# Sixteen weight tiles, each loaded as 120 partitions and 8 partitions

## The chip, the cores and the metric

The kernel runs on one core of a Trainium2 chip. The metric is the device time of one execution in microseconds (us), the median over several runs. The core has a matrix engine (TensorE, PE in the profile), VectorE (DVE), ScalarE (ACT), GpSimd (POOL) and a queue engine SyncE (SP). Sixteen DMA engines carry all transfers between the memory of the chip (HBM) and the on-chip memory of 128 partitions (SBUF). Transfers are issued from SP, from ACT or from POOL, and all go to the same sixteen engines.

## The reference

One sequence of 256 tokens, width 1024, float32 all through, goes through two transformer blocks. The first has a gated feed-forward network, a token mixer (gated linear attention and blocked softmax attention) and another feed-forward network. The second has a mixer of a gated delta rule and an mLSTM, cross-attention to 256 memory tokens, and at its end a layer of 16,384 single-row experts (PEER). The change is in that last layer:

```
q = (rmsnorm(h, w) @ wq) as 8 heads of 2 x 128
scores of each half against 128 sub-keys; the 16 best of each half; the 16 best of their 256 sums -> 16 expert ids for each head and token
h += sum over heads and their 16 ids of  gate * act(u[id] . x) * v[id]
```

The weight `peer_wq` (1024 x 2048) gives the queries. Each token picks 8 x 16 = 128 experts, and each expert has one row u and one row v of 1024 floats, stored side by side as one row of `peer_uv`.

## The kernel before

Each engine has one instruction stream, written out in order by Python when the kernel is built. Buffers and semaphore counts are planned at that time too.

**Weights.** Almost all weights come as tiles of 128 partitions x 1024 floats (512 KB, one row of 4 KB for each partition), issued by SP in one list. The last part of that list is `TAIL` (line 181 of the code): 8 tiles of the second mixer's output weight, 8 of the cross-attention query weight, 8 of its output weight, and from index `T_PQ` = 24 on the 16 tiles of `peer_wq`. `PLACE[i]` says in which buffer tile i lands (`tail_slot(i)`), `FREED[i]` which earlier tile held that buffer. SP waits until that one has been used, and then issues one transfer (line 2874). A tile's semaphore is one of 16, `tail{i % NLAND}`. `land(...)` books 16 counts for a transfer, and `at(...)` gives the count that stands for it.

**The expert layer.** Tokens are worked on in two halves of 128 (r = 0, 1) and 8 heads: sixteen steps q = 8 r + head. `peer_tile(q)` (line 1216) multiplies the normed tokens with two tiles of `peer_wq` (indices 24 + 2 head and 25 + 2 head) into PSUM, 16 matmuls. It waits for each tile's semaphore. The tiles stay in place for the second half of the tokens. `peer_keys(q)` scores the sub-keys, and VectorE picks the sixteen expert ids.

**The gathers.** For each q and each of its 16 ids, POOL issues an indirect DMA (line 2831) which brings one row of `peer_uv` (8 KB) for each of the 128 tokens into one of nine buffers. There are 256 gathers. VectorE multiplies the u half with the token and sums (line 2131), ScalarE makes a gate and writes a diagonal matrix (line 2700), and TensorE adds the diagonal times the v half to an accumulator, four passes of 512 columns with weight loads (line 1313). That frees the buffer, and POOL issues a gather into it. The order of all this on TensorE and VectorE is the list of `peer_order()`. The routing of step q + 1 and later (tile, keys, top 16) is slotted between the gathers of step q. The matmul of line 1133 belongs to the output projections before it (the mixer's, the cross-attention's), and in part still runs beside the first gathers.

**The order at the change.** SP issues the 16 tiles of `peer_wq` as the buffers come free, while the cross-attention ends and the first gathers run. After them SP has only the output to write.

Of the kernel before, what the change touches and what calls it, by code (L numbers as in the profile page):

```python
# [23 lines left out]
NLAND = 16  # L24
# [9 lines left out]
class Book:  # L34
# [23 lines left out]
    def land(self, name, *key):  # L58
        return self.step(name, key, 16)

    def at(self, name, *key):
        return self.sem(name), 1 if self.known is None else self.known[(name,) + key]
# [119 lines left out]
T_OUT, T_XQ, T_XO, T_PQ = 0, 8, 16, 24  # L182
# [87 lines left out]
def program(nc, D, out, stack, book):  # L270
    up, at, land = book.up, book.at, book.land
# [147 lines left out]
    def raw_slot(j):  # L419
        return raw[:, (j % NRAW) * SLOT:(j % NRAW + 1) * SLOT]  # L420
# [5 lines left out]
    def tail_slot(i):  # L426
        k = PLACE[i]
        if k < NRAW:
            return raw_slot(items + k)
        if k >= 14:  # L430
            return extra[k]
        k -= NRAW
        return (whi32, wlo32)[k // NSPL][:, k % NSPL * SLOT:(k % NSPL + 1) * SLOT]
# [2411 lines left out]
    def sync_engine():  # L2845
        s = nc.sync
        for j, (kind, name, *i) in enumerate(stream):
            if j >= NRAW:
                k = j - NRAW
                if stream[k][0] == "w":  # L2850
                    s.wait_ge(*at("lo", k))
                elif stream[k][0] == "mod" and stream[k][2] == 0 and stream[k][3] < NMOD:
                    s.wait_ge(*at("ada_t", "shift", stream[k][3]))
                elif stream[k][0] in SUMS:
                    s.wait_ge(*at("ada", k))
                else:
                    s.wait_ge(*at("br", 2 * (raws.index(k) // 2) + 1))
            src = D[name][GATES.index(i[0]), i[1]] if kind == "ada" else D[name][MODS.index(i[0]), i[1]] if kind == "mod" else D[name][i[0]]
            s.dma_start(raw_slot(j), src).then_inc(*land(f"raw{j % NRAW}", j))
        for i, (name, _, k) in enumerate(TAIL):  # L2860
            j = FREED[i]
            if i < NRAW:
                s.wait_ge(*at("lo", items + i - NRAW))
            elif PLACE[i] < 14 and j is None:
                s.wait_ge(*at("tile", split_at[len(split_at) - 1 - (len(split_at) - 1 - (PLACE[i] - NRAW)) % NSPL]))
            elif j is None:
                s.wait_ge(*at("stage_t", 1, 0))
            elif j % 4 < 3:
                s.wait_ge(*at("used", j))
            elif T_XQ <= j < T_XO:  # L2870
                s.wait_ge(*at("xa_t", "q", 1, (j - T_XQ) // 4))
            else:
                s.wait_ge(*at("rows", "xa" if j >= T_XO else "mixed", j // 4 % 2, 1))
            s.dma_start(tail_slot(i), D[name][k]).then_inc(*land(f"tail{i % NLAND}", i))
        o3 = out.rearrange("(r p) n -> p r n", p=128)
        for r in range(2):
            for n in range(2):
                c = slice(n * 512, (n + 1) * 512)
                s.wait_ge(*at("last", r, "out") if n else at("last_sq", r, "out"))
                s.dma_start(o3[:, r, c], h[:, r, c]).then_inc(*land("out", r, n))  # L2880
        s.wait_ge(*at("out", 1, 1))
# [3 lines left out]
    scalar_engine()  # L2885
    gpsimd_engine()
    sync_engine()


# [131 lines left out]
```

## Time and profile before

| | us |
|---|---|
| median of 3 runs (lowest, highest) | 1637.08 (1636.48, 1638.92) |
| span of the profiled execution | 1635.0 |
| TensorE busy | 1492.0 (91%) |
| VectorE busy | 1054.2 (64%) |
| ScalarE busy | 721.3 (44%) |
| GpSimd busy | 332.9 (20%) |
| chain of waits: share of TensorE, of DMA | 57%, 24% |

The span runs from the first to the last instruction of the profiled execution. The device time of a run has some two microseconds around it. The page divides the span into 40 slices of 40.9 us and gives the busy share of each engine in tenths. The DMA line is the mean over the sixteen DMA engines. In the chain of waits each piece is what released the next, back from the last instruction.

### The profile page before, as it was taken

The numbers are of one execution on the slowest core, as the hardware profiler recorded it, in microseconds if no ns is written. First come the engines' busy times: TensorE is split into PE (matmuls) and PEld (weight loads), VectorE is DVE, ScalarE is ACT, GpSimd is POOL, SyncE is SP. The second block draws the span as 40 slices with busy tenths as digits, with TensorE's granted clock in tenths as the row PEclk, the third lists the DMA queues.
The fourth block names the chain that finished last, engine by engine and source line by source line (L and its number), as shares of the span: only waits on it lengthen the run. The fifth ranks groups of instructions, "written<-read, shape, count | busy, mean of one in ns | idle before, by whom it ended". The sixth has DMA issues, their size and how long they took to land.

```text
span 1635.0 us, 21410 instructions
## 1 busy us (share of the span) xinstructions
PE 1492.0 (91%) x7868; PEld 1099.5 (67%) x7868; DVE 1054.2 (64%) x1959; ACT 721.3 (44%) x1579; POOL 332.9 (20%) x324
## 2 busy tenths in 40 slices
PE   6999999999999999999999989988988888888786
PEld 6899998889899998999996665444433433334222
DVE  5677775756666556659652276667677677676644
ACT  4445455454454345645331243444444444444443
POOL 0200010000010001000001033434444444444441
PEclk9999999999999999899999999999999999999999
DMA  8989884447567656333325379999999999999995
GB/s 327 393 284 315 290 308 136 155 122 278 206 200 236 219 186 215 121 117 108 103 87 196 139 320 338 404 421 420 422 421 421 420 422 421 422 421 421 419 422 239
DMA packets 91738, 470.48 MB, mean 288 GB/s; under 512 B 10864, under 2 KB 11024, under 8 KB 58096
## 3 DMA queue, kind: packets, MB, share of 16 engines
q0 software_dynamic: 40096, 284.39, 42.7%
q1 hardware_dynamic: 50688, 183.52, 32.5%
q8 instruction: 63, 1.03, 0.3%
q10 hardware_dynamic: 848, 1.18, 0.2%
q14 instruction: 43, 0.35, 0.1%
HBM read 462.51 MB, written 4.46 MB: 286 GB/s over the span
## 4 chain that ended last, share of the span: by engine, by line
PE 57%; DMA 24%; DVE 8%; ACT 7%; issue 3%; POOL 0%; SPq 0%; ACTq 0%; DVEq 0%; POOLq 0%
DMA Ft<-peer_uv,ids 18%; PE ps L1313 8%; PE ps L519 7%; PE ps L521 7%; PE ps L520 7%; PE ps L1133 3%; DMA mlo<-peer_uv,ids 3%; DVE Ft L2131 3%; PE ps L644 2%; PE ps L645 2%; PE ps L646 2%; PE ps L563 2%; PE ps L564 2%; PE ps L565 2%; PE ps L859 2%
## 5 line engine op out<-in xcount | busy, mean ns | idle before, releaser
L1313 PE MATMUL ps<-Ft 128*128 128x512 f32 x792 | 385.9, 622 | 80.1 <-ACT Ft L2700 79.4
L1313 PEld LDWEIGHTS ps<-Ft 128*128 128x128 f32 x792 | 145.4, 195 | 298.1 <-ACT Ft L2700 167.7
L2131 DVE CUSTOM_DVE_ANT_0 Ft<-Ft 128x1024 f32<-128x1024 f32 x198 | 242.6, 1225 | 147.7 <-DMA Ft<-peer_uv,ids 140.0
L1341 DVE TENSOR_TENSOR wlo<-raw,whi 128x1024 fp32r<-128x1024 f32 x228 | 274.8, 1228 | 81.8 <-ACT whi L2155 81.3
L519 PE MATMUL ps<-uhi,whi 128*128 128x256 f32 x1088 | 314.1, 289 | 8.5 <-DVE wlo L1341 5.2
L520 PE MATMUL ps<-ulo,whi 128*128 128x256 f32 x1088 | 310.2, 285 | 0.0
L521 PE MATMUL ps<-uhi,wlo 128*128 128x256 f32 x1088 | 310.1, 285 | 0.0
L2831 POOL DMA_INDIRECT Ft<-peer_uv,ids x198 | 216.6, 1094 | 298.8 <-PE ps L1313 272.5
L2155 ACT ACTIVATE whi<-raw 128x1024 fp32r<-128x1024 f32 x228 | 232.0, 1049 | 34.4 <-DMA raw<-ff_gu 9.2
L519 PEld LDWEIGHTS ps<-uhi,whi 128*128 128x128 f32 x1088 | 211.1, 194 | 12.9 <-issue 6.0
L520 PEld LDWEIGHTS ps<-ulo,whi 128*128 128x128 f32 x1088 | 211.1, 194 | 2.1 <-issue 0.7
L521 PEld LDWEIGHTS ps<-uhi,wlo 128*128 128x128 f32 x1088 | 210.9, 194 | 0.0
L2694 ACT ACTIVATE Ft<-Ft 128x1 f32<-128x1 f32 x256 | 51.7, 202 | 346.7 <-DVE Ft L2131 346.2
L2700 ACT ACTIVATE Ft<-Ft 128x128 f32<-128x128 f32 x256 | 102.7, 401 | 8.3
L2276 ACT ACTIVATE Ft<-ps 128x256 f32<-128x256 f32 x44 | 16.9, 383 | 160.9 <-PE ps L521 160.9
L2697 ACT ACTIVATE Ft<-Ft 128x1 f32<-128x1 f32 x256 | 75.4, 294 | 8.3
L644 PE MATMUL ps<-whi,mhi 128*128 128x512 f32 x176 | 70.2, 399 | 0.9 <-DVE wlo L1341 0.9
L1556 DVE TENSOR_TENSOR Ft<-ps,Ft 128x256 f32<-128x256 f32 x44 | 18.6, 424 | 79.2 <-ACT Ft L2276 79.2
L645 PE MATMUL ps<-wlo,mhi 128*128 128x512 f32 x176 | 69.6, 395 | 0.0
L646 PE MATMUL ps<-whi,mlo 128*128 128x512 f32 x176 | 69.0, 392 | 0.0
L1313 PE MATMUL ps<-mlo,Ft 128*128 128x512 f32 x116 | 58.3, 626 | 11.5 <-ACT Ft L2700 11.3
L1313 PE MATMUL ps<-uhi,Ft 128*128 128x512 f32 x116 | 56.5, 610 | 10.6 <-ACT Ft L2700 10.4
(457 smaller groups left out, 2192.5 us busy)
## 6 DMA issues: line engine op xcount, KB each, us to landing
raw<-ff_gu SPq DMA_DIRECT2D x88, 512.0 KB, 4.7
raw<-w_mod SPq DMA_DIRECT2D x48, 512.0 KB, 5.3
raw<-ff_dn SPq DMA_DIRECT2D x44, 512.0 KB, 5.1
raw<-w_in SPq DMA_DIRECT2D x32, 512.0 KB, 3.7
raw<-w_in_s SPq DMA_DIRECT2D x28, 512.0 KB, 3.7
raw<-w_ada SPq DMA_DIRECT2D x24, 512.0 KB, 5.9
raw<-w_out SPq DMA_DIRECT2D x14, 512.0 KB, 4.0
raw<-w_in_m SPq DMA_DIRECT2D x12, 512.0 KB, 3.6
```

Source lines behind the costliest of these rows:

```text
L519: t.matmul(o, hi[:, c], x[0][:, i], start=(k == 0), stop=False)
L520: t.matmul(o, hi[:, c], x[1][:, i], start=False, stop=False)
L521: return t.matmul(o, lo[:, c], x[0][:, i], start=False, stop=(k == 7))
L644: t.matmul(acc[n, r], m[0][:, c], a, start=(f == 0), stop=False)
L645: t.matmul(acc[n, r], m[0][:, c], b, start=False, stop=False)
L646: return t.matmul(acc[n, r], m[1][:, c], a, start=False, stop=(f == 21))
L1313: ins = t.matmul(acc[r][c], diag[n % NDIAG], gbuf[SEAT[n]][:, 1024 + c * 512:1024 + (c + 1) * 512], start=False, stop=(n % 128 == 127))
L1341: v.tensor_tensor(lo, raw_slot(j), hi.bitcast(F32), ALU.subtract).then_inc(*up("lo", j))
L2131: v.tensor_tensor_reduce(pjunk, gbuf[SEAT[n]][:, 0:1024], xn[:, q // 8, :], 1.0, 0.0, ALU.mult, ALU.add, dots[:, n:n + 1]).then_inc(*up("d ...
L2155: a.activation(split_slot(j)[0], raw_slot(j), ACT.Copy).then_inc(*up("hi", j))
L2700: a.activation(diag[n % NDIAG], ident, ACT.Copy, scale=wgt[:, c]).then_inc(*up("diag", n))
L2831: p.indirect_dma_start(gbuf[SEAT[n]], None, D["peer_uv"], bass.IndirectOffsetOnAxis(ap=ids[:, n:n + 1], axis=0)).then_inc(*land(f"gather{S ...
```

## The change

The transfers of tiles 24 to 39, which are the sixteen of `peer_wq`, are each issued as two: partitions 0 to 119, and right behind it partitions 120 to 127. Both count up the same semaphore by 16. The count under the tile's own key is now that of the second one, so whoever waits for the tile waits for both. The wait of SP before the tile, the buffers and the order are as before.

```diff
-            s.dma_start(tail_slot(i), D[name][k]).then_inc(*land(f"tail{i % NLAND}", i))
+            if i < T_PQ:
+                s.dma_start(tail_slot(i), D[name][k]).then_inc(*land(f"tail{i % NLAND}", i))
+            else:
+                s.dma_start(tail_slot(i)[0:120], D[name][k][0:120]).then_inc(*land(f"tail{i % NLAND}", i, "most"))
+                s.dma_start(tail_slot(i)[120:128], D[name][k][120:128]).then_inc(*land(f"tail{i % NLAND}", i))
```

## Rows read from the trace of the kernel before

**Rows 1.** The page: busy tenths in 40 slices, and the DMA rate.

```profile
PE   6999999999999999999999989988988888888786
...
DMA  8989884447567656333325379999999999999995
GB/s 327 393 284 315 290 308 136 155 122 278 206 200 236 219 186 215 121 117 108 103 87 196 139 320 338 404 421 420 422 421 421 420 422 421 422 421 421 419 422 239
```

**Rows 2.** Stretches: length, busy us (count) of PE, PEld, DVE, ACT, POOL; clock, DMA share, GB/s.

```profile
980.00:1000.00 20.00, 18.41 (x97) 12.54 (x96) 4.79 (x8) 4.62 (x15) 6.66 (x7) 1.00 0.91 317
...
1020.00:1055.00 35.00, 35.00 (x111) 17.80 (x110) 21.27 (x54) 14.84 (x44) 16.24 (x15) 1.00 1.00 401
1055.00:1612.00 557.00, 467.34 (x1293) 208.88 (x1293) 381.98 (x909) 244.25 (x740) 241.35 (x220) 0.98 1.01 421
```

**Rows 3.** The chain of waits around 1055 us: start, length, what.

```profile
1051.44 3.45 PE ps L1313 x8
...
1055.15 21.29 DMA Ft<-peer_uv,ids
...
1081.51 18.10 DMA Ft<-peer_uv,ids
```

**Rows 4.** The DMA view of 1613 to 1626 us, forty slices of 0.325 us.

```profile
DMA  9998754333311211100010000000000000000000
GB/s 429 429 403 353 328 252 202 151 151 151 126 76 50 101 50 76 50 25 25 25 25 0 25 25 25 25 25 25 25 25 25 25 25 25 25 0 0 0 0 0
```

**Rows 5.** The timeline at the end: start, length, instruction, idle before it and releaser.

```profile
1622.49 1.23 DVE L2131 CUSTOM_DVE_ANT_0 Ft<-Ft 128x1024 f32<-128x1024 f32 x1 [2.21 <-DMA Ft<-peer_uv,ids]
...
1624.95 1.23 DVE L2131 CUSTOM_DVE_ANT_0 Ft<-Ft 128x1024 f32<-128x1024 f32 x1 [1.23 <-DMA Ft<-peer_uv,ids]
```

**Rows 6.** SP's timeline, its issues of peer_wq (neighbours merged, x is their count).

```profile
912.19 0.43 SPq L2874 DMA_DIRECT2D Ft<-peer_wq  x1
929.93 0.33 SPq L2874 DMA_DIRECT2D raw<-peer_wq  x1
932.09 16.89 SPq L2874 DMA_DIRECT2D whi<-peer_wq  x4
950.44 3.90 SPq L2874 DMA_DIRECT2D wlo<-peer_wq  x3
...
1026.86 0.33 SPq L2874 DMA_DIRECT2D wlo<-peer_wq  x1
1034.17 33.50 SPq L2874 DMA_DIRECT2D raw<-peer_wq  x5
1067.71 0.43 SPq L2874 DMA_DIRECT2D Ft<-peer_wq  x1
```

**Rows 7.** The DMA view of 1055 to 1612 us: queues; issues, KB each, us to landing.

```profile
q8 instruction: 10, 0.16, 0.1%
q14 instruction: 17, 0.14, 0.1%
...
raw<-peer_wq SPq DMA_DIRECT2D x2, 512.0 KB, 7.8
Ft<-peer_wq SPq DMA_DIRECT2D x1, 512.0 KB, 11.2
```

**Rows 8.** SP's waits over the span: us in total, times, longest.

```profile
SPq L2880 <- ACT Ft L2663: 562.1, 2, 318.7
```

**Rows 9.** The chain of waits between 925 and 985 us.

```profile
937.38 3.34 DMA whi<-peer_wq
```

**Rows 10.** The DMA view of the span: a transfer of 4 KB.

```profile
Ft<-norm_final_col POOLq DMA_DIRECT2D x1, 4.0 KB, 2.9
```

**Rows 11.** The DMA view of 910 to 960 us: the second tile.

```profile
raw<-peer_wq SPq DMA_DIRECT2D x1, 512.0 KB, 3.3
```

**Rows 12.** TensorE's timeline where it first reads the second tile.

```profile
933.68 1.95 PE L1216 MATMUL ps<-ulo,raw 128*128 128x128 f32 x16
```

**Rows 13.** The view of peer_wq: who waited for its transfers (us, times).

```profile
  PEld ps L1216: 0.3, 1
```

## The prediction

> **What bounds the kernel now.** I read the page from the top. TensorE is busy for 91% of the span, but in the last fifteen of the forty slices its digit falls to 8 and then 7, while the line of the DMA engines stands at 9 and the rate at 420 to 422 GB/s without a dip [rows 1]. The table of stretches says it sharper: between 1055 and 1612 us the sixteen DMA engines are busy for a share of 1.01 at 421 GB/s, TensorE for 467 of 557 us, VectorE for 382 [rows 2]. That stage is the gather of the expert rows: each gather brings 128 rows of 2048 floats, 8 KB each, 1.05 MB together, and 1.05 MB at 421 GB/s is 2.49 us. The chain of waits agrees. Until 1054.9 us it runs through the matmuls of line 1313 and others on TensorE; from 1055.15 on it is nearly all one thing, a gather in flight for 18 to 21 us, a few microseconds of VectorE, ScalarE and TensorE that free its buffer, and the next gather [rows 3]. So in this stage only the bytes on the DMA engines count, and more exactly the bytes on the engine that finishes last.
>
> That engine is visible. The rate over 1613 to 1626 us is given in forty slices of 0.325 us [rows 4]. One engine alone moves 421/16 = 26.3 GB/s. The rate falls to 151, then 50 (two engines), and from slice 17, that is from 1618.5 us, it is 25 until slice 34, 1624.4 us. So fifteen engines have delivered their share of the last gather by about 1618.5 us, and one goes on by itself for 5.9 us, with one gap. VectorE waits for it: its last two dot products start at 1622.49 and 1624.95 us, each right behind a DMA wait, and the rest of the kernel is a fixed tail from there to 1635.0 us [rows 5]. The second-latest engine ends at 1618.5, the third at about 1617. The share of 1.01 before says that no engine rested, so these lags are differences in the work that each engine had, and any work taken from the late engine moves the end until the second-latest binds.
>
> **The change, part by part.** Sixteen loads of 512 KB, one row of 4 KB for each of 128 partitions, become 32: 120 rows, then 8. Bytes are the same. What moves is on which engines they go. Whole, a load gives each of 16 engines 8 rows. 120 is fifteen times 8; the other 8 rows are the share of one engine. I take it that the 120 rows go to fifteen engines, 8 each as before, that the last engine has none, and that the 8 rows of the second transfer go one each to the first eight engines. No row of the trace before shows a transfer from SP that isn't of 128 partitions, so this is an assumption with rivals below.
>
> Where it counts: a load matters to the end only if it lands while the engines have no rest. Of the sixteen, nine are issued between 912 and 954 us, before the stage [rows 6]; there, TensorE and VectorE carry the chain and a shift of the engines' work is lost when they next idle (their share is still 0.91 between 980 and 1000 us [rows 2]). Seven are issued from 1026.86 to 1067.71 us, where the share is 1.00 and then 1.01. Before 1055 the chain is TensorE's, but the queue that builds up there is not emptied again, so I count all seven; the lower bound is three, those that landed after 1055 as the view of transfers has it [rows 7].
>
> Price of a row: 4096 bytes at 26.3 GB/s is 0.156 us. The spared engine loses 7 x 8 x 0.156 = 8.7 us of work (with three loads 3.7 us). Each of the first eight gains 7 x 0.156 = 1.09 us (0.47 us).
>
> If the late engine is the spared one: its lead over the second-latest, 5.9 us, is smaller than 8.7, so the second-latest binds. That one is among the first eight, and then 1.09 us later, or not: I take half, 0.55 us. The third, 1.5 us earlier, stays behind it even with 1.09. Gain 5.9 - 0.55 = 5.3 us. With the lower bound of three loads it would be 3.7 us.
>
> **What is added on the path.** (a) SP issues 16 more transfers of 0.33 to 0.43 us each [rows 6], 5 to 7 us in all. Behind them SP waits only for the next buffer and then, 562 us in all, for the output [rows 8], so that is free but where a tile is awaited. (b) Awaited is one: the fourth tile, issued at 937.38 us, stands in the chain for 3.34 us [rows 9] and holds TensorE for 0.3 us. Its second part is issued 0.33 us later. The nearest row for a tiny transfer is one of 4 KB that landed 2.9 us after its issue [rows 10]. So the tile is complete at 0.33 + 2.9 = 3.2 us, no later, or at 3.34 + 0.43 = 3.8 us. The range is -0.1 to +0.45 us; I take 0.3, nearer the upper end, since 8 rows queue behind the first part on their engines. The second tile, issued at 929.93, landed 3.3 us later and was used at 933.68 [rows 11, 12]: 0.4 us to spare, so it may add 0.1 at most. The chain from there on is TensorE, ScalarE and VectorE, so the 0.3 us is passed on to the start of the DMA stage. (c) All later tiles have microseconds between landing and use: that one wait of 0.3 us is all that is listed for the sixteen [rows 13]. If that cover went, it would cost what (b) costs, 0.3 us apiece. (d) Each of the first eight engines has a second completion write for each load. It costs less than a row of 4 KB, so between 0 and 1.09 us for the seven; I take 0, as the sixteen that each gather has now leave the rate at 421 GB/s. (e) TensorE, VectorE and ScalarE execute the same instructions, and the semaphore of a tile is waited for at its new full count, so nothing else moves.
>
> The Trainium skill bears on the assumption: "DMA: Bandwidth & Descriptors", "Why a DMA increments its semaphore by 16 and not by 1", says that a transfer from SP runs on the largest number of engines up to 16 that divides its partitions, the lowest-numbered ones, which is 15 for 120 and 8 for 8. No row here shows it. The Trainium skill's same page, under "Rules for kernel authors", says not to bother with two transfers over disjoint partitions, as they share the same engines; by that rule alone the change would be worth nothing or the cost of (b), but it speaks of halves, each of which sprays over all sixteen.
>
> **Sum.** -5.9 + 0.55 + 0.3 = -5.0 us on the profiled span of 1635.0. The median is 1637.08, so 2.1 us lie around the span and stay. Prediction 1637.1 - 5.0 = 1632.1 us. Its own range is 1630.8 (second-latest engine not among the first eight, no slip, a little more for the earlier loads) to 1633.9 (three loads count, or every cost at its upper end).
>
> **The rivals.** What can be told from no change is about 0.2%, 3.3 us.
>
> 1. The late engine is one of those that are not touched, or the eight rows fall to the same engine that had them before (the second transfer starting where the first left off). Then only the slip is left: 1637.1 + 0.3 = 1637.4 us. For it: no row names the late engine. Against it: the cut is just where one engine's share begins. Chance 0.16.
>
> 2. The late engine is among the first eight. Then it is late by 1.09 us more: 1637.1 + 1.1 + 0.3 = 1638.5 us, later than before. By count alone eight of sixteen engines would speak for this. Chance 0.18.
>
> 3. 120 rows are dealt to fewer engines, eight with 15 rows each, because 16 doesn't divide 120. Then the first eight engines have 16 rows in place of 8 of each load, 7 x 8 x 0.156 = 8.7 us more. If the late one is not among them, the end is that of the latest of the eight, which was up to 5.9 us ahead: +2.8 us; if it is, +8.7 us. 1640 to 1646 us, slower. It decides from the first load in the stage. Against it: 120 divides by fifteen, and 8 rows an engine is what a whole load has. Chance 0.09.
>
> 4. The forecast: the late engine is the spared one. Chance 0.57. The reason from the rows is that one engine stands alone by 5.9 us while the others end within some 4 us of each other [rows 4]: it has something extra that is tied to one engine. What other traffic the stage has is the two instruction queues, 0.1% each [rows 7], and 0.1% of all sixteen engines' time over 557 us is 9 us if one engine bears it. That such a duty sits on the engine at the end of the row rather than on one in its midst is a guess, and with it goes more than half of my confidence.
>
> The Trainium skill, "DMA: Bandwidth & Descriptors", "Latency and other measured facts", says that DMA engines 7 and 15 are usually slower than the rest, with a best guess as the cause. The trace agrees that some are slower, one by 5.9 us and a second by 1.5 us over the third; which two is not shown. If 15 is the later one, the change gives the forecast; if 7 is, rival 2.
>
> **How the numbers follow.** Faster by over 0.2% needs a gain of 3.3 us: nearly all of case 4 (0.52 of 0.57), none of the others. Slower by over 0.2% needs case 3, or case 2 with twice the slip: 0.10. The rest, 0.38, is within 0.2%. The range that holds 8 in 10 runs from 1630.7 to 1639.5: it takes in case 4, 1 and 2 and leaves out case 3. The likeliest case has 1630.8 to 1633.9.
>
> **What would show it.** In the profile after: at the end of the stage, the rate in slices falls to 25 GB/s for no more than 1.5 us, and the last two dot products start 2.5 us apart at about 1617.5 and 1620; the share up to there stays at 1.01. The time from the last dot product to the end of the span stays 10.0 us. SP shows 32 issues of peer_wq, and the wait of TensorE for the fourth tile grows from 0.3 to 0.6 us. Rival 1 keeps the lone engine at 5.9 us, rival 2 lengthens it to 7, rival 3 shows eight engines (210 GB/s) at the end. The prediction is wrong if the lone engine stays, or if it goes and the dot products are held by something else.

## The result, and the profile after

The changed kernel takes 1654.4 us (median of 4; 1651.2 to 1657.0) against 1636.8 us (median of 4; 1635.9 to 1638.9): 17.6 us more, ratio 1.0114 with a 95% interval of 1.0097 to 1.0131. I had forecast 1632.1 us and a range up to 1639.5. It is slower, and by more than any rival named: the dearest, the third, ended at 1646 us. The ratios in this document are those of the record; they need not equal the quotient of the two medians to the last digit.

The profiled execution after the change has a span of 1655.6 us (its time, 1656.95, is the highest of the four). Its page, the lines that answer to [rows 1]:

```profile
PE   6999999999999999999999989878988898888786
...
DMA  8989884546666556333335299999999999999996
GB/s 327 364 293 309 294 306 133 160 125 264 216 211 234 203 189 227 111 102 115 103 102 216 77 317 383 331 356 421 420 421 421 420 421 420 422 421 421 421 421 251
```

Busy tenths and rate part here. In the 26th and 27th slice (1035 to 1118 us) the DMA engines stand at 9, but the rate is 331 and 356 GB/s where it was 404 and 421. The table of stretches says how much (columns as in [rows 2]). First the kernel after the change:

```profile
1020.00:1055.00 35.00, 34.58 (x116) 17.78 (x114) 19.10 (x42) 13.58 (x41) 14.28 (x15) 1.00 0.99 337
1055.00:1090.00 35.00, 26.18 (x56) 10.23 (x56) 20.07 (x54) 12.82 (x37) 10.28 (x10) 0.95 1.02 326
1090.00:1130.00 40.00, 31.53 (x96) 14.96 (x95) 26.93 (x70) 13.77 (x45) 14.82 (x13) 0.91 1.01 389
1130.00:1610.00 480.00, 403.13 (x1124) 182.65 (x1123) 331.88 (x796) 212.97 (x644) 219.90 (x194) 0.97 1.01 421
```

and the same view of the kernel before, for the stretches that [rows 2] has not got:

```profile
1055.00:1090.00 35.00, 29.47 (x98) 14.35 (x98) 22.95 (x59) 14.92 (x45) 11.60 (x12) 1.00 1.02 420
1090.00:1130.00 40.00, 34.06 (x100) 15.99 (x99) 29.07 (x73) 18.32 (x57) 17.75 (x17) 0.96 1.01 421
```

A share of 1.02 with 326 GB/s means that every engine always has a packet under way and that each packet takes longer. The DMA view of 1020 to 1110 us has the two queues apart: packets, MB, share of the sixteen engines' time. Queue q0 carries the gathers, q1 SP's loads. Before the change, then after it:

```profile
q0 software_dynamic: 4584, 33.41, 90.4%
q1 hardware_dynamic: 1008, 3.67, 10.2%
```

```profile
q0 software_dynamic: 3661, 26.67, 86.4%
q1 hardware_dynamic: 1057, 3.67, 14.0%
```

Share times 16 x 90 us, divided by the number of 8 KB or 4 KB packets in those MB, gives the time of one: a gather's packet goes from 319 to 382 ns, a row of a load from 164 to 225 ns. The gathers, which nobody changed, are slowed too. From 1020 to 1130 us the engines brought 337 x 35 + 326 x 35 + 389 x 40 = 38.8 MB where they had brought 401 x 35 + 420 x 35 + 421 x 40 = 45.6 MB. The 6.8 MB have to be made up at 421 GB/s, which takes 16.2 us. That is most of the loss. From 1130 us on the rate is 421 again: what stretches the packets comes and goes with the seven loads. SP issues them in this profile from 1033.31 to 1082.88 us:

```profile
1033.31 0.33 SPq L2877 DMA_DIRECT2D wlo<-peer_wq  x1
1033.68 0.31 SPq L2878 DMA_DIRECT2D wlo<-peer_wq  x1
...
1082.51 0.33 SPq L2877 DMA_DIRECT2D Ft<-peer_wq  x1
1082.88 0.30 SPq L2878 DMA_DIRECT2D Ft<-peer_wq  x1
```

In the chain of waits, one gather of this time is in flight for 29.39 us, where [rows 3] had 21.29 and 18.10:

```profile
1038.99 20.81 DMA Ft<-peer_uv,ids
...
1067.93 29.39 DMA Ft<-peer_uv,ids
...
1102.38 19.07 DMA Ft<-peer_uv,ids
```

The two spans differ by 20.6 us, so 4.4 us are left. They lie ahead of 1020 us: between 950 and 1020 us the rate is 340 GB/s after the change and 365 before it, 1.75 MB or 4.2 us less, and the gathers had started 3.6 us late. Of these 3.6 us, the profiled execution was late by 2.6 us already at SP's load of the cross-attention tiles, ahead of anything changed (884.75 us against 882.13), and 1.0 us came between there and the first gather (951.71 against 948.13). In that stretch the second tile stands in the chain and TensorE waits for two of its tiles, 2.4 us in all where [rows 13] had 0.3: 0.9 us for the second and 1.5 us for the fourth. (In the view the same two waits stand twice, once for the weight load, PEld, and once for the matmul, PE.) The chain of waits, then, from the view of the tiles, who waited for their transfers:

```profile
932.55 0.33 SPq L2877
...
932.92 4.19 DMA raw<-peer_wq
```

```profile
  PEld ps L1216: 2.4, 2
  PE ps L1216: 2.0, 2
```

At the end, the lines that answer to [rows 4] and [rows 5]: the DMA view of 1633 to 1646 us in slices of 0.325 us, and VectorE's timeline.

```profile
DMA  9999999987444434221111200010000000000000
GB/s 403 429 429 429 403 454 403 403 353 302 202 176 202 176 126 151 101 101 76 76 50 50 50 25 25 25 50 25 25 25 25 25 25 25 25 25 25 0 0 0
```

```profile
1643.16 1.23 DVE L2131 CUSTOM_DVE_ANT_0 Ft<-Ft 128x1024 f32<-128x1024 f32 x1 [2.21 <-DMA Ft<-peer_uv,ids]
...
1645.62 1.23 DVE L2131 CUSTOM_DVE_ANT_0 Ft<-Ft 128x1024 f32<-128x1024 f32 x1 [1.22 <-DMA Ft<-peer_uv,ids]
```

The lone engine is still there: 25 GB/s from 1640.5 to 1645.0 us, but for one slice of 50, so it stands alone for 4.5 us. The tail from the last dot product to the end is 10.0 us as before.

### The profile page after: what moved, and what is told of

Same layout as the page of the kernel before. It is cut to its first block, busy times and chain, and to the rows that moved or that the text cites. A ratio compares the mean times of both kernels' runs of the same rounds, so it can differ in the third digit from the quotient of the medians.

```text
span 1655.6 us, 21426 instructions
## 1 busy us (share of the span) xinstructions
PE 1500.9 (91%) x7868; PEld 1102.7 (67%) x7868; DVE 1054.7 (64%) x1959; ACT 722.0 (44%) x1579; POOL 339.2 (20%) x324
## 4 chain that ended last, share of the span: by engine, by line
PE 56%; DMA 26%; DVE 8%; ACT 6%; issue 3%; POOL 1%; SPq 0%; ACTq 0%; DVEq 0%; POOLq 0%
DMA Ft<-peer_uv,ids 20%; PE ps L1313 8%; PE ps L519 7%; PE ps L521 7%; PE ps L520 7%; DMA mlo<-peer_uv,ids 3%; PE ps L1133 3%; DVE Ft L2131 3%; PE ps L644 2%; PE ps L645 2%; PE ps L646 2%; PE ps L563 2%; PE ps L564 2%; PE ps L565 2%; PE ps L859 2%
## 5 line engine op out<-in xcount | busy, mean ns | idle before, releaser
L1313 PE MATMUL ps<-Ft 128*128 128x512 f32 x792 | 390.5, 628 | 91.1 <-ACT Ft L2700 90.7
L2831 POOL DMA_INDIRECT Ft<-peer_uv,ids x198 | 224.4, 1133 | 314.4 <-PE ps L1313 287.2
```

The costliest lines, as they stand in the source:

```text
L1313: ins = t.matmul(acc[r][c], diag[n % NDIAG], gbuf[SEAT[n]][:, 1024 + c * 512:1024 + (c + 1) * 512], start=False, stop=(n % 128 == 127))
L2831: p.indirect_dma_start(gbuf[SEAT[n]], None, D["peer_uv"], bass.IndirectOffsetOnAxis(ap=ids[:, n:n + 1], axis=0)).then_inc(*land(f"gather{S ...
```

## The experiments

All differences are between medians, against the kernel before on the same chip. To compare them by one view, each has its stretch of 1020 to 1130 us, in which the last seven tiles are loaded. The theories are named by letters; what each says is in the expectation that first names it. The kernels before and after in that view, one fence each:

```profile
1020.00:1130.00 110.00, 98.54 (x305) 48.14 (x304) 73.29 (x184) 48.08 (x144) 45.59 (x43) 0.98 1.01 414
```

```profile
1020.00:1130.00 110.00, 92.29 (x266) 42.97 (x265) 66.09 (x166) 40.17 (x122) 39.38 (x37) 0.95 1.01 353
```

Theory W, whose direction stood in the end while its sizes came out only roughly: a load of all 128 partitions deals its rows to the engines as a gather does; any other load deals them otherwise, so that engines meet on the way into the on-chip memory. It was first put more narrowly, as theory P, for the fifteen engines of a 120-row transfer.

**Another cut, sixteen engines in both parts.**

```diff
+                s.dma_start(tail_slot(i)[0:112], D[name][k][0:112])...
+                s.dma_start(tail_slot(i)[112:128], D[name][k][112:128])...
```

> The sixteen query tiles are split at partition 112 in place of 120, so that both parts (112 = 16 x 7 rows, 16 = 16 x 1 row) divide over sixteen engines. Theory P (what costs 17.6 us is that a transfer of 120 rows runs on fifteen engines and puts its rows elsewhere than a whole one, which stretches the packets of all engines beside the gathers): 0 to +3 us against before, packets of the gathers back at 314 ns, rate back at 421 GB/s. Theory N (two transfers in place of one cost this, whatever their sizes): +15 to +18 us. Theory S (the short second transfer): 0 to +3 us, since its rows are spread one to an engine.

Measured: 1649.2 against 1636.0 us, +13.2 us, ratio 1.0074 (1.0052 to 1.0096).

```profile
1020.00:1130.00 110.00, 93.08 (x260) 42.88 (x259) 66.63 (x161) 44.73 (x133) 43.48 (x40) 0.95 1.01 371
```

Theory P fell: it had named 0 to 3 us, and 112 rows, a number that sixteen divides, are nearly as dear as 120. It is not fifteen engines as such.

**The first transfer alone.**

```diff
+            n = 128 if i < T_PQ else 120
+            s.dma_start(tail_slot(i)[0:n], D[name][k][0:n])...
```

> Only partitions 0 to 119 of the sixteen query tiles are loaded, in one transfer each; the rows 120 to 127 keep what was there, so the queries and the chosen experts are other ones. Theory P: +14 to +18 us against before, rate of 300 to 345 GB/s while these loads are in flight. Theories S and N: the cost is gone, -1 to +1 us.

Measured: 1647.1 us, +11.1 us, ratio 1.0073 (1.0050 to 1.0097), below the 14 that P had named. Theories N and S fall: one transfer in place of one, fewer bytes, and most of the loss. The stretch and then the DMA view of 1622 to 1635 us:

```profile
1020.00:1130.00 110.00, 93.66 (x261) 43.07 (x259) 65.61 (x159) 44.06 (x131) 43.62 (x40) 0.95 1.01 371
```

```profile
GB/s 403 403 454 403 378 403 479 378 328 302 302 302 277 227 202 151 202 126 101 101 126 76 50 0 0 25 25 25 25 25 25 25 25 25 25 50 25 0 0 0
```

The second view bears on the forecast: one engine is again alone at the end, here for some 4 us, though no engine has anything extra and one engine, if 120 rows are fifteen shares, has 8.7 us less. So the late engine is not the one spared, if the rows are dealt that way; no view shows how they are dealt.

**Only the last seven tiles.** The edit of the change with `i < 33` in place of `i < T_PQ`.

> Only the last seven query tiles (index 33 to 39), those issued while the gathers keep the DMA engines without rest, are split 120 + 8; the first nine are whole. All theories that put the loss into the stage of the gathers expect nearly all of it: +14 to +18 us. If the first nine carry a part (tiles that are awaited, first gathers held up), it is +8 to +13 us.

Measured: 1650.4 us, +14.4 us, ratio 1.0090 (1.0070 to 1.0110); the rate in the stretch is 361 GB/s. So 14.4 of the 17.6 us are in the seven loads beside the gathers. The difference of 3.2 us for the first nine compares two chips and is no closer than a microsecond or two.

**Whole loads, and eight rows again.**

```diff
+                s.dma_start(tail_slot(i), D[name][k])...(i, "whole")
+                s.wait_ge(*at(f"tail{i % NLAND}", i, "whole"))
+                s.dma_start(tail_slot(i)[120:128], D[name][k][120:128])...
```

> All tiles are loaded whole; for the last six (index 34 to 39) SP then waits for the landing and loads partitions 120 to 127 once more, with the same rows. Theory S (the eight rows on eight engines cost): +10 to +16 us. Theories P and N (by the form of the 120-row transfer): 0 to +2 us, 6 x 0.156 = 0.9 us of it the added rows.

Measured: 1638.9 us, +3.0 us, ratio 1.0021 (1.0011 to 1.0030), above the 2 us that P and N had named and far below the 10 of S.

```profile
1020.00:1130.00 110.00, 95.97 (x298) 46.73 (x297) 70.51 (x178) 46.93 (x141) 47.96 (x43) 0.98 1.01 405
```

The eight rows are the smaller part, but 0.5 us for each 32 KB is three times what the bytes cost. The lost rate accounts for most of it, as with the other cuts: (414 - 405) x 110 / 421 = 2.4 us of lost rate.

**Cuts at 64 and 96.** As the first edit, with 64 and 96.

> The sixteen query tiles are split at partition 64: two transfers of 64 rows, 4 rows for each of sixteen engines, one after the other over the same half of the partitions. Theory W (any transfer that isn't the whole 128 deals its rows to the engines otherwise than the gathers do, so that engines write to the same part of the on-chip memory at the same time): as dear as 120 + 8 or dearer, +11 to +22 us, packets of the gathers well over 350 ns on the mean beside these loads. Theory K (a cost of row counts such as 7 and 8 in a block, or of a first part that leaves few rows for the second): 64 is a power of two and even, 0 to +4 us.

> The split is at partition 96: 6 rows and 2 rows for each of sixteen engines. Theory W: +8 to +18 us. Theory K: 0 to +4 us.

Measured: 64 + 64 1649.8 against 1635.6 us, +14.2 us, ratio 1.0087 (1.0070 to 1.0104); 96 + 32 1649.6 us, +14.0 us, ratio 1.0073 (1.0054 to 1.0092). Theory K falls. W's ranges hold, but not its "as dear as 120 + 8 or dearer" for 64 + 64: that was 17.6 us. Their rates in the stretch are 363 and 368 GB/s. With 64 + 64 a gather's packet takes 369 ns on the mean, worked out as above; W had said over 350.

**Copies from HBM to HBM, without rows.** Behind each of the last seven tiles, loaded whole, a second transfer of its 128 or 120 rows into a scratch area in HBM.

> All tiles are loaded whole as before, and behind each of the last seven its 128 rows are copied once more from HBM to a scratch area in HBM, which nobody reads. This is the control of the next: 7 x 8 rows x 0.156 us = 8.7 us for every engine if a row to HBM costs what a row to the on-chip memory costs, and up to +20 us if writing to HBM is slower.

> As the control, but only rows 0 to 119 are copied from HBM to HBM. Theory W (the collision is at the write into the on-chip memory): the same as the control within 2 us, as fifteen engines have the same 8 rows each. Theory R (it is the reading, the generator of the descriptors, or fifteen engines as such): 10 to 18 us more than the control.

Measured: 1645.4 and 1644.4 against 1635.6 us, +9.7 and +8.8 us, ratios 1.0056 (1.0039 to 1.0073) and 1.0053 (1.0037 to 1.0070). It looks like a verdict for W and is none. The packets in the trace are of 32 KB and 30 KB: source and target were both without gaps, and the transfer went as sixteen pieces. The DMA view (1020 to 1110 us) of the control shows it by the count of packets under 8 KB, 1567, where the kernel before has 1514 and seven copies in rows would have added 896:

```profile
DMA packets 5343, 37.37 MB, mean 415 GB/s; under 512 B 671, under 2 KB 671, under 8 KB 1567
```

**The same with rows.** The scratch area gets a row pitch of 4608 bytes.

```diff
+                s.dma_start(D["copy"][i - 33][0:120, 0:1024], D[name][k][0:120])...
```

> The copies to HBM of the earlier pair went as 16 pieces of 32 KB or 30 KB and not as rows, so they did not have the form in question. Here the scratch area has a row pitch of 4608 bytes, so that a copy is made of rows of 4 KB. Control: 128 rows copied behind each of the last seven tiles. 7 x 8 rows x 0.156 us = 8.7 us: +8 to +12 us for both theories.

> As the control, 120 rows, which fifteen engines carry. Theory W (the collision is at the write into the on-chip memory): the same as the control within 3 us, packets of the gathers at 314 to 330 ns, one engine ahead of the rest. Theory R (reading from HBM, the descriptors, or fifteen engines as such): 8 to 14 us more than the control, packets stretched as in the run with 120 rows only.

Measured: 128 rows 1644.9 against 1635.5 us, +9.3 us, ratio 1.0055 (1.0038 to 1.0071); 120 rows 1643.8 us, +8.3 us, ratio 1.0046 (1.0029 to 1.0063). The control's DMA view (1020 to 1110 us) now has 2465 - 1567 = 898 small packets more, which is 7 x 128 rows and two; then the stretch of the 120-row run:

```profile
DMA packets 6134, 37.42 MB, mean 416 GB/s; under 512 B 673, under 2 KB 673, under 8 KB 2465
```

```profile
1020.00:1130.00 110.00, 93.33 (x267) 43.24 (x266) 68.28 (x170) 45.79 (x136) 46.67 (x42) 0.98 1.01 418
```

The rate stays at 418 GB/s beside the 120-row copies, a gather's packet takes 317 ns, and the copies cost about their bytes: 8.7 us by the forecast's own price. The same rows read from the same place in HBM by the same queue do no harm when they aren't written to the on-chip memory. Theory R falls.

**Eight transfers of 16 rows, neighbouring or spaced.**

```diff
+                for g in range(8):
+                    p = slice(16 * g, 16 * g + 16)     # second kernel: slice(g, 128, 8)
+                    s.dma_start(tail_slot(i)[p], D[name][k][p])...
```

> Each of the last seven tiles is loaded in eight transfers of 16 neighbouring partitions, one row for each of sixteen engines. If rows are dealt in order and four neighbouring partitions share one way into the memory, four engines meet at each of four ways: a row there takes 4 x 0.156 us in place of 0.156, so 8 x 7 x 0.47 = 26 us, and with the factor 1.5 by which the measured costs of the other splits exceed such a count, up to 40: Theory W +26 to +40 us. A theory that counts transfers or packets alone: the same as the next run.

> The same eight transfers of 16 rows for each of the last seven tiles, but the rows of one are eight partitions apart (0, 8, 16, ... and so on), so only two engines meet at one way. Theory W: 8 x 7 x 0.156 = 8.7 us, with the factor 1.5 up to 14: +8 to +15 us, less than half of the run before. A theory that counts transfers or packets alone: the same as the run before.

Measured: neighbouring 1661.2 against 1635.5 us, +25.7 us, ratio 1.0145 (1.0128 to 1.0162); spaced 1650.5 us, +15.0 us, ratio 1.0091 (1.0074 to 1.0107).

```profile
1020.00:1130.00 110.00, 88.15 (x238) 42.26 (x237) 57.67 (x143) 36.96 (x112) 34.62 (x34) 0.91 1.01 320
```

```profile
1020.00:1130.00 110.00, 89.76 (x257) 41.33 (x255) 63.80 (x157) 44.34 (x132) 50.59 (x40) 0.98 1.02 367
```

Both have the same number of transfers, rows, packets and bytes. What differs is which partitions one transfer fills, and with it 10.7 us; a theory that counts transfers or packets alone falls. One thing more differs: a tile lies in HBM without gaps, so the first kernel reads sixteen neighbouring rows in a transfer and the second every eighth row. No copy to HBM was made in groups of sixteen rows, so it isn't excluded that the reading has a part in the 10.7 us. W had the order right and its sizes only roughly: 25.7 us lies just under the 26 to 40 that it named, 15.0 us at the end of its 8 to 15, and the second is more than half of the first, where it had said less. The ratio is 1.7, where the plain count gives 3.

The Trainium skill, "SBUF — State Buffer", "Door 1: The DMA port swizzle", has a way in for every four neighbouring partitions, shared with the four that lie 32 above, and "DMA: Bandwidth & Descriptors", "The descriptor swizzle", has each engine of a 128-partition transfer write one such way alone. The trace agrees with what follows from the two: in the stretch of 1020 to 1130 us, 414 GB/s beside whole loads and 320 beside groups of 16 neighbouring partitions. That engines meet at such a way is not seen in any view; it is argued from these rates. How rows are dealt in a transfer of another size no view of the profile shows; that they go in order is the assumption under W's counts.

## Why the prediction was wrong

**What bounds the kernel: right.** From 1055 us on only the DMA engines count: the 6.8 MB that were missing by 1130 us are 16.2 of the 20.6 us by which the span grew, with the tail at 10.0 us as before.

**"What moves is on which engines they go ... 8 each as before" (the change part by part): this step failed.** I priced a row at 4096 bytes over 26.3 GB/s = 0.156 us, wherever it goes and whatever runs beside it. That price holds for a whole load and for the copies to HBM (8.7 us named, 9.3 and 8.3 measured). It does not hold for a load of part of the partitions into the on-chip memory: with only the last seven tiles cut the kernel lost 14.4 us, 2.1 us for each tile, where the sum had a gain of 5.3 us and no term for a loss on all engines. The rows before the change showed no such transfer; I wrote that down as an assumption and bounded only which engines carry the rows, from 0 to 16 rows each, and not what a row costs there. With no row near it, the price of such a load should have widened the range upward.

**"If the late engine is the spared one": not borne out.** With 120 rows alone one engine still ends by itself. The gain of 5.3 us did not show even there. Which engine is late, and whether it is among the first eight, stays open. The forecast also read the third-latest engine too early: [rows 4] has 76 GB/s, three engines, at 1618 us and not 1617, so it was some 0.5 us behind the second-latest and not 1.5. And the time around the span is 1.2 to 1.4 us in every run whose span was recorded; the rest of the 2.1 us that the forecast put there is the distance from the profiled execution to the median. Neither matters beside 17.6 us.

**The rivals.** The first (the late engine is not touched) and the second may have had the engine right, and had no term for the loss. The third, the slower one, named 1640 to 1646 us by eight engines of 15 rows. In the profile it would have shown some engines idle and others full; in fact all are full at a lower rate. Its sign was right, its mechanism wrong.

The rule of the Trainium skill ("DMA: Bandwidth & Descriptors", "Rules for kernel authors") against two transfers over disjoint halves, which I set aside, was right in its advice: the cut at 64 cost 14.2 us. The reason that it gives, that both parts share the same engines, would by itself have cost nothing here.

**The awaited tiles.** Predicted were 0.3 us of slip and 0.6 us of waiting; TensorE waited 2.4 us, and 1.0 us of slip reached the first gather. The second tile, to which I gave 0.4 us to spare, was the one in the chain: it took 4.56 us from its first issue where it had taken 3.3 [rows 11].

**SP's issues and the packets of completion** cost nothing that these runs can tell apart: eight transfers for each of seven tiles in spaced partitions cost 15.0 us, two of 64 rows for each of sixteen 14.2. The rows go to other partitions in the two, so this isn't a clean test.

## What to carry to other kernels

Beside a stream that fills the DMA engines, load into all 128 partitions in one transfer: loads that cover part of them cost about 2 us for each 512 KB beyond their bytes, whether cut at 120, 112, 96 or 64. Read the DMA busy share and the rate together. A full share with a rate under the usual one, at packets of the same sizes, means that packets are being stretched, and then it is the form of the transfers in flight to look at and not their number. A price taken from bytes over bandwidth is safe only for transfers of a form that the trace already has: of two new forms here, the copies to HBM cost about their bytes and the loads to part of the partitions did not.

## What the runs showed of the hardware

- Loads to part of the partitions lower the rate of the sixteen engines together while they are in flight, from about 420 to 326 GB/s in the stretch from 1055 to 1090 us, at a busy share of 1.02.
- Eight 16-row transfers for each of seven tiles cost 25.7 us with neighbouring partitions in each and 15.0 us with partitions eight apart; the rows read in HBM are neighbours or eight apart with them.
- Rows copied from HBM to HBM beside the gathers cost about their bytes: 9.3 us for 3.7 MB at 128 rows and 8.3 us for 3.4 MB at 120, with 417 and 418 GB/s in the stretch. Without gaps on both sides such a copy goes as sixteen packets of 32 KB.
- Unexpected and unexplained: between 925 and 950 us, with hardly a gather in flight, 480 KB over 120 partitions took 4.3 us to land (the run of the first transfer alone), 448 KB over 112 partitions 3.5 us, and 512 KB whole 3.6 us before the change and 3.9 us in the run with eight rows again (medians of three or four loads each).
- One DMA engine ends 4 to 6 us after all others in each of the three profiles whose end is shown here.
